# First layer norm of the experts' half: contiguous rows, one token tile at a time through its own banks, router by tile

## The reference

```
mix = hybrid_mixer(x, ...)                                  # three kinds of attention, then w_o
x   = layer_norm(ALPHA * x + mix, ln1_g, ln1_b)             # the first norm: this is what is changed
lg  = x @ router_group_w + b;   le = x @ router_expert_w + b   # 4 + 32 = 36 logits a token
...                                                         # best group, its two best experts, gates
moe = sum over chosen experts of (silu(x @ w_gate) * (x @ w_up)) * gate @ w_down
x   = layer_norm(ALPHA * x + moe, ln2_g, ln2_b)
```

## Time and profile before

| | |
|---|---|
| median of three runs | 1674.71 us |
| profiled execution, first to last instruction (its span; its own time is given only as this) | 1670.3 us |
| PE busy | 1640.6 us, 98% |
| PE weight loads busy | 1241.8 us, 74% |
| DVE busy | 856.1 us, 51% |
| ACT busy | 651.0 us, 39% |
| POOL busy | 172.6 us, 10% |
| mean granted TensorE clock | 0.996 of full speed |

### The profile page before, as it was taken

How to read it: one execution, slowest core, us unless ns; L and a number is a source line. 1 busy time by engine, 2 the same in 40 slices (tenths; PEclk the granted TensorE clock), 3 DMA queues, 4 the chain that set the end, 5 groups by cost and what they waited for, 6 DMA issues and landing times. The chain is left out here.

```text
span 1670.3 us, 23474 instructions
## 1 busy us (share of the span) xinstructions
PE 1640.6 (98%) x9386; PEld 1241.8 (74%) x9386; DVE 856.1 (51%) x1420; ACT 651.0 (39%) x920; POOL 172.6 (10%) x242
## 2 busy tenths in 40 slices
PE   9999999999999999999999999999999999999997
PEld 7888879999798887999988976444448887544443
DVE  6566564444646556544456867322117785532223
ACT  5455444343445454433345453111115455211111
POOL 2020001111102100111111040000002022000000
PEclk9999999999999999999999999999999999999999
DMA  9544545553654455465546546999996637699996
GB/s 324 184 140 151 177 152 182 196 178 124 229 181 146 151 176 177 153 199 177 180 157 196 189 142 230 406 422 420 421 392 211 193 126 250 228 421 421 421 417 260
DMA packets 158589, 396.61 MB, mean 237 GB/s; under 512 B 20753, under 2 KB 85265, under 8 KB 140049
## 3 DMA queue, kind: packets, MB, share of 16 engines
q1 hardware_dynamic: 158480, 395.18, 65.0%
HBM read 394.10 MB, written 1.05 MB: 237 GB/s over the span
## 5 line engine op out<-in xcount | busy, mean ns | idle before, releaser
L948 PE MATMUL ps<-split,split 128*128 128x256 f32 (+3 forms) x1872 | 631.7, 337 | 0.6 <-issue 0.3
L952 PE MATMUL ps<-split,split 128*128 128x256 f32 (+3 forms) x1872 | 627.8, 335 | 0.6 <-DVE split L2707 0.6
L949 PE MATMUL ps<-split,split 128*128 128x256 f32 (+3 forms) x1872 | 623.9, 333 | 0.0
L926 DVE TENSOR_TENSOR split<-ring,split 128x2048 fp32r<-128x2048 f32 x136 | 312.5, 2305 | 254.0 <-ACT split L919 253.9
L952 PEld LDWEIGHTS ps<-split,split 128*128 128x128 f32 x1872 | 352.0, 188 | 36.1 <-DVE split L2412 1.1
L948 PEld LDWEIGHTS ps<-split,split 128*128 128x128 f32 x1872 | 351.8, 188 | 35.3 <-issue 2.4
L949 PEld LDWEIGHTS ps<-split,split 128*128 128x128 f32 x1872 | 353.2, 189 | 33.0 <-issue 0.5
L919 ACT ACTIVATE split<-ring 128x2048 fp32r<-128x2048 f32 x136 | 260.3, 1915 | 278.0 <-PE ps L952 267.8
L1874 PE MATMUL ps<-ring,arena 128*64 128x512 f32 x464 | 105.8, 592 | 0.3 <-DMA ring<-in_expert_w_up 0.3
L3068 DVE SCALAR_TENSOR_TENSOR arena<-arena,ps 128x256 f32<-128x256 f32 x32 | 15.4, 480 | 171.7 <-ACT arena L2327 136.0
L1874 PE MATMUL ps<-arena 128*64 128x512 f32 x288 | 99.5, 594 | 0.0
(11 more groups left out here) (260 smaller groups left out, 1690.5 us busy)
## 6 DMA issues: line engine op xcount, KB each, us to landing
ring<-in_w_in SPq DMA_DIRECT2D x52, 1024.0 KB, 5.1
ring<-in_w_gate_up SPq DMA_DIRECT2D x44, 1024.0 KB, 5.3
ring<-in_expert_w_down SPq DMA_DIRECT2D x32, 1024.0 KB, 13.2
ring<-in_w_down SPq DMA_DIRECT2D x22, 1024.0 KB, 5.0
ring<-in_w_in SPq DMA_DIRECT2D x28, 768.0 KB, 4.5
ring<-in_expert_w_gate SPq DMA_DIRECT2D x20, 1024.0 KB, 11.9
ring<-in_expert_w_up SPq DMA_DIRECT2D x20, 1024.0 KB, 14.0
arena<-in_expert_w_down SPq DMA_DIRECT2D x16, 1024.0 KB, 14.5
```

The source lines that it names most:

```text
L926: nc.vector.tensor_tensor(split(slot), slot, split(high[:, n % HIGH, :]), ALU.subtract).then_inc(low_done.sem, 1)
L948: nc.tensor.matmul(acc, sh, mh, start=start, stop=False)
L949: nc.tensor.matmul(acc, *second, start=False, stop=False)
L952: return nc.tensor.matmul(acc, *third, start=False, stop=stop)
```

## The change

`Z` is now written as it is read, row for row, without the step of eight. The step is moved to where PE reads `Z`, `H_high` and `H_low` as stationary operands (`k::KT`), in the transposes and in the gathers. Each token tile is turned into four banks of its own (4 to 7 for tile 0, 1 to 4 for tile 1), the blocks are taken out 128 columns at a time, and the router takes the tiles one after the other. A table `Z_BY` says which engine takes which block: ACT (0) takes k = 0 to 5 of tile 0 and k = 2, 3, 6, 7 of tile 1, DVE (1) the rest. PE runs 6 filler matmuls instead of 16, and its order becomes: turn tile 0, router for blocks 0 to 5 of tile 0, turn tile 1, router for blocks 6 and 7 of tile 0, router for tile 1. `shift` is computed on POOL. In DVE's queue the memsets and the two blocks of tile 0 stand ahead of the normalisation of tile 1; in ACT's queue the six blocks of tile 0 stand ahead of the split of `Z[:, 0]`. The residual in duos 1 and 3 loses its step.

```diff
+Z_BY = ((0, 0, 0, 0, 0, 0, 1, 1), (1, 1, 0, 0, 1, 1, 0, 0))
...
-    out += [(("xT2", kp), 4 + kp) for kp in range(4)] + [(("router", 0), 0), (("ranks", 0), 1)]
+    out += [(("xT2", 0, kp), 4 + kp) for kp in range(4)] + [(("xT2", 1, kp), 1 + kp) for kp in range(4)]
+    out += [(("router", 0), 0), (("ranks", 0), 1)]
...
+            def turn_z(t, l):
+                done = (z_act, z_dve)[t]
+                pe.wait_ge(done.sem, done.at(l, 1))
+                for k in range(KT):
+                    key = ("xT2", t, k // 2)
+                    acc = claim2(key, l) if k % 2 == 0 else bank2(key)
+                    mm = nc.tensor.transpose(acc[:, k % 2 * P:(k % 2 + 1) * P], Z[:, t, k::KT], ident[:])
+                    if k % 2 == 1:
+                        fill(mm, key)
+            def route(t, first, last, l):
+                acc = bank2(("router", 0))
+                for k in range(first, last + 1):
+                    engine, n = z_block(t, k)
+                    signal_ = (xT2_act, xT2_dve)[engine]
+                    pe.wait_ge(signal_.sem, signal_.at(l, n))
+                    mm = nc.tensor.matmul(acc[:, t * 64:t * 64 + 36], T8[:, k, t * P:(t + 1) * P], rw[:, k, :],
+                                          start=(t == 0 and k == 0), stop=(t == TT - 1 and k == KT - 1))
...
-                keep_running(bank2(("xT2", 3)), 16)
-                turn_z(l)
-                (router: for each k the matmuls of both tiles)
+                keep_running(bank2(("xT2", 0, 3)), 6)
+                turn_z(0, l)
+                route(0, 0, 5, l)
+                turn_z(1, l)
+                route(0, 6, 7, l)
+                route(1, 0, 7, l)
...
-                                                      moe_split((H_high, H_low)[part][:, t, k * P:(k + 1) * P]),
+                                                      moe_split((H_high, H_low)[part][:, t, k::KT]),
...
-                nc.scalar.activation(in_blocks(Z[:, 0, :]), H[:, 0, :].rearrange("p (n k) -> p k n", k=KT), ACT.Identity,
-                                     scale=rstd2[:, 0:1], bias=shift[:, 0:1]).then_inc(z_act.sem, 1)
+                nc.scalar.activation(Z[:, 0, :], H[:, 0, :], ACT.Identity, scale=rstd2[:, 0:1],
+                                     bias=shift[:, 0:1]).then_inc(z_act.sem, 1)
+                leave_z(0)
                 act.wait_ge(z_act.sem, z_act.at(l, 1))
                 high_of_z(0)
-                (the blocks k = 0, 1, 4, 5 of both tiles)
+                leave_z(1)
...
-                    if i == 3:
-                        dve.wait_ge(rstd_done.sem, rstd_done.at(l, 1))
-                        nc.vector.scalar_tensor_tensor(out=shift, in0=mv2[:, 0, 0:1], scalar=-1.0, in1=rstd2[:, 0:1],
-                                                       op0=ALU.mult, op1=ALU.mult).then_inc(shift_in.sem, 1)
...
+                (memsets)
+                leave_z(0)
+                dve.wait_ge(rstd_done.sem, rstd_done.at(l, 2))
+                nc.vector.tensor_scalar(Z[:, 1, :], H[:, 1, :], mv2[:, 1, 0:1], rstd2[:, 1:2], ALU.subtract,
+                                        ALU.mult).then_inc(z_dve.sem, 1)
+                leave_z(1)
+                low_of_z(0)
...
-                                out=H[:, d // 2, :].rearrange("p (n k) -> p n k", k=KT),
-                                in0=Z[:, d // 2, :].rearrange("p (k n) -> p n k", k=KT), scalar=ALPHA,
-                                in1=lng[:, 0, :].rearrange("p (n k) -> p n k", k=KT), op0=ALU.mult,
+                                out=H[:, d // 2, :], in0=Z[:, d // 2, :], scalar=ALPHA, in1=lng[:, 0, :], op0=ALU.mult,
...
+                    if t == 0:
+                        pool.wait_ge(rstd_done.sem, rstd_done.at(l, 1))
+                        nc.gpsimd.tensor_scalar(shift, mv2[:, 0, 0:1], rstd2[:, 0:1], -1.0, ALU.mult,
+                                                ALU.mult).then_inc(shift_in.sem, 1)
```

More of the change, by code:

```diff
@@ L273, in gathers_in, with z_block @@
     return [(g, n)] if group_parts(g) == 4 else [(g, 2 * n), (g, 2 * n + 1)]
+def z_block(t, k):
+    engine = Z_BY[t][k]
+    return engine, sum(Z_BY[i][j] == engine for i in range(TT) for j in range(KT) if (i, j) <= (t, k))
 def gather_banks(d):
@@ L697, in build @@
         bT_low = signal("bT_low", 16)
-        xT2_act = signal("xT2_act", 4)
-        xT2_dve = signal("xT2_dve", 4)
+        xT2_act = signal("xT2_act", sum(row.count(0) for row in Z_BY))
+        xT2_dve = signal("xT2_dve", sum(row.count(1) for row in Z_BY))
         u_act = signal("u_act", 10)
@@ L767, in wait_apart @@
             eng.sem_inc(passed, 1)
-        def in_blocks(view):
-            return view.rearrange("p (k n) -> p k n", k=KT)
         def bank_of(key):
@@ L809, in build @@
             read2["xT", kp] = (bT_low, kp + 5)
-            read2["xT2", kp] = ((xT2_act, xT2_dve)[kp % 2], 2 * (kp // 2) + 2)
+            for t in range(TT):
+                engine, n = z_block(t, 2 * kp + 1)
+                read2["xT2", t, kp] = ((xT2_act, xT2_dve)[engine], n)
             read2["uq", kp] = (mq_in, kp + 1)
@@ L1588, in turn_stream @@
                             fill(mm, ("xT", b))
[L1590 to L1599, removed]
+            def turn_z(t, l):
[15 more added lines that the diff above has]
+                                          start=(t == 0 and k == 0), stop=(t == TT - 1 and k == KT - 1))
+                if t == TT - 1:
+                    fill(mm, ("router", 0))
             def index_scores(h, l):
@@ L2280, in high_of_z, with leave_z @@
                     nc.scalar.activation(moe_split(H_high[:, t, :]), Z[:, t, :], ACT.Copy).then_inc(split_high.sem, 1)
+                def leave_z(t):
+                    for k in range(KT):
+                        engine, _ = z_block(t, k)
+                        if engine == 0:
+                            acc = content2(("xT2", t, k // 2), l)
+                            nc.scalar.activation(T8[:, k, t * P:(t + 1) * P], acc[:, k % 2 * P:(k % 2 + 1) * P],
+                                                 ACT.Identity, scale=ln1_of_d[:, 0, k:k + 1],
+                                                 bias=ln1_of_d[:, 1, k:k + 1]).then_inc(xT2_act.sem, 1)
                 act.wait_ge(shift_in.sem, shift_in.at(l, 1))
-                nc.scalar.activation(in_blocks(Z[:, 0, :]), H[:, 0, :].rearrange("p (n k) -> p k n", k=KT), ACT.Identity,
-                                     scale=rstd2[:, 0:1], bias=shift[:, 0:1]).then_inc(z_act.sem, 1)
+                nc.scalar.activation(Z[:, 0, :], H[:, 0, :], ACT.Identity, scale=rstd2[:, 0:1],
+                                     bias=shift[:, 0:1]).then_inc(z_act.sem, 1)
+                leave_z(0)
                 act.wait_ge(z_act.sem, z_act.at(l, 1))
                 high_of_z(0)
[L2287 to L2290, removed]
+                leave_z(1)
                 act.wait_ge(z_dve.sem, z_dve.at(l, 1))
@@ L2927, in _, with leave_z @@
                                                 ALU.add).then_inc(stat_done.sem, 1)
[L2928 to L2935 removed]
+                def leave_z(t):
+                    for k in range(KT):
+                        engine, _ = z_block(t, k)
+                        if engine == 1:
+                            acc = content2(("xT2", t, k // 2), l)
+                            nc.vector.tensor_scalar(T8[:, k, t * P:(t + 1) * P], acc[:, k % 2 * P:(k % 2 + 1) * P],
+                                                    ln1_of_d[:, 0, k:k + 1], ln1_of_d[:, 1, k:k + 1], ALU.mult,
+                                                    ALU.add).then_inc(xT2_dve.sem, 1)
                 nc.vector.memset(minus_mean, -1.0 / D)
```

20 lines of the change are left out of this document (3 added, 17 removed).

## The result

| | before | after |
|---|---|---|
| median | 1674.71 us (1673.34 to 1675.06, 5 runs) | 1707.08 us (1704.22 to 1710.50, 5 runs) |
| span of the profiled execution | 1670.3 us | 1702.4 us |
| mean granted clock | 0.996 | 0.990 |

The change made the kernel slower, by the ratio 1.0196, 95% interval 1.0185 to 1.0208: 32.4 us where 2.0 us were to be won.

A forecast was written before the change was run, and what follows sets the result against it. PE, busy 98% of the span, was taken as the bound, with DMA also full in the duos. Router 1.23 us sooner less 0.2 for gathers: 1.0 a layer, 2.0 in both, 1674.7 - 2.0 = 1672.7 us; range 1670.9 to 1675.4.

The forecast's parts named there:

- Gathers with a step of eight: PE's gathers reading weights with a step: 32 narrow ones on the path cost nothing to 0.6 us a layer, 0.2 taken.
- Rival A: The step slows PE's gathers by x us each; 1679.2 us with the longer load, about 1699 if the rate halves; 5%.
- the halving: PE's gather rate halves under the step as ACT's does, x = 0.12: 12 us a layer, about 1699 us; one percent.
- Rival B: Low clock comes in both layers and falls on the first duo, losing 1.7 us each: 1676.1 us; 7%.
- Shift on POOL: Normalisation of tile 0: shift computed on POOL is ready at 7.37, so ACT can start at 7.40 instead of 8.26.
- rows without a step: ACT's normalisation of tile 0 read and written contiguously takes 1.2 us instead of 2.23; tile 1's on DVE 0.85.
- transposes: PE's transposes of Z with a step of eight stay about as fast, 0.124 us apart.
- blocks: ACT takes out six 128-column blocks of tile 0, 0.355 us apart, done at 11.37; DVE's two are done at 10.77.
- router: PE's router instructions, 0.112 us apart, end at 15.05 instead of 16.28: 1.23 us sooner a layer.
- D: Rival: PE hardly waits for ACT's 128-column blocks (distance nearer 0.25 than 0.355 us), gain 3.5 to 4.2, about 1670.9 us; 13%.
- I take the shift of the first gather as the shift of the layer's end: Time won before the gathers reaches the layer's end in full, once per layer, the DMA stretch moving along.
- Hidden: DVE's residual in duos 1 and 3 loses its step, without effect on the time, as DVE is busy 47 of 196 us.

The follow-up runs named there:

- e1: The changed kernel with the gathers' stationary operands contiguous again (wrong columns, same sizes): 1675.67 us, ratio 1.0003 to the kernel before.
- e2: The kernel before with only a step of eight put into the gathers' stationary operands (wrong columns): 1709.29 us, ratio 1.0213 to the kernel before.
- e3: The changed kernel with the step of eight only in each layer's first 32 narrow gathers, later ones contiguous: 1687.67 us, ratio 1.0078 to the kernel before.
- e5: The changed kernel with a step of four instead of eight in the gathers' weights (wrong columns): 1704.53 us, ratio 1.0178 to the kernel before.
- e6: The changed kernel with both halves written in column blocks, the high one by ACT, so gathers are contiguous and right: 1680.94 us, ratio 1.0041 to before.
- e7: The changed kernel with halves written in column blocks, the high one by POOL instead of ACT, gathers contiguous and right: 1678.85 us, ratio 1.0029 to before.
- g1: The changed kernel, but rows normalised in blocks as before, gathers contiguous and right, ten fillers, other DVE order: 1677.31 us, ratio 1.0018 to before.
- the small kernel: Separate kernel, run once, with groups of 24 matmuls varying type and step of the weights: fp32r at 160 columns, step 8, takes 5.96 us.

## Why the prediction was wrong, point by point

- **The step that failed** is "*Gathers with a step of eight*": "The nearest rows for the step are again the transposes, where it adds 0.002 to 0.019 to the distance ... I take 0.2". The mechanism was named there, that the weight load sets the distance; its rate under a step was taken from rows that do not show it. It adds 0.135 us at 160 columns and 0.249 - 0.151 = 0.098 at 320 (20 in 5.16 us against 3.19). The rows of the load itself were among those read, 198 ns against 141, and were called latency. In the gathers the same reading went from 190 to 335 ns.
- **Rival A** had it: with x = 0.12 "about 1699". With the measured 0.135 and 0.098 the same sum is 32 x 0.135 + 96 x 0.098 + 32 x 0.135 = 18.0 a layer, less 1.3 won and the waits of 1.7 and 2.4 us taken back: some 29.5 in both, 1704. The low clock in the first duos, 2.4 in both, and the 2 us between the layers come on top and would make 1708 to 1709; 1707.08 was measured. Its "covered up to about 2 us by the wait for DMA" held. The weight of one in a hundred on the halving was wrong, against a row of ACT that showed it and the rule of the Trainium skill that the prediction itself names; the prediction let one kind of PE instruction speak for another.
- **Rival B** had the low clock in both layers and in the first duo. It came, for 10 us and not 3.4, and with e1 it went. The four profiles whose first gathers are slow (the changed kernel, e2, e3, e5) have it at them in both layers, for 7 to 10 us; of the ten others it stands at the first gathers in three of 20 layers (e6, e7, g1). So the slow gathers bring it, though they are not the only thing that does. It cost 1.1 to 1.3 a layer, nearly all of it behind the gathers, for with a step of eight these are no slower at 1.2 GHz (0.248) than those of the small kernel at full clock (0.247). In e2, where the clock falls in the middle of them, they start 0.242 us apart at full clock and 0.241 at half. This holds for the slow load alone: contiguous gathers start 0.113 apart at full clock and 0.214 at half (g1). Without the step the low clock still came more often, and there it took gain.
- **Shift on POOL, rows without a step, transposes, blocks, router**: right to 0.1 us each on PE's path; 1.23 forecast, 1.30 measured. ACT's row at 128 columns, where D had its hope, was as computed: six in 2.20 against 2.23.
- **"I take the shift of the first gather as the shift of the layer's end"**: right for a delay (e3), and not so for a gain. "If PE is earlier, the releases are" did not hold in full, since e1's waits for weights grew by 1.2 us; and it left out that a stage can be shorter and still bring the low clock oftener. In e1 this took the gain (1675.67 against the 1672.7 forecast); in the changed kernel the step decided.
- **Hidden**: the residual fell from 1956 to 1215 ns a row, and nothing else moved with it, as said.

## What to carry to other kernels

A layout change moves a step from one reader to another, so price it at every reader, and at TensorE price the load of the weights and not only the matmul: ask at each matmul whether the load or the columns set the distance. Where the nearest row is of another kind of instruction, a minute with a small kernel that varies only the step would have told a loss of 2% from a gain of 0.1%. When a gain of a microsecond doesn't arrive, sort single runs by their granted clock as well as looking for a new wait.

## What the runs showed of the hardware that was not expected

- The load of 128 x 128 fp32r weights takes 0.118 us contiguous, 0.126 at step 2, 0.181 at 3, 0.244 at 4 and 0.247 at 8; 24 bf16 loads with 64 columns each take 0.86 us contiguous and at step 2, 0.95 at step 4, 1.61 at step 8. Transposes of fp32 blocks stay at 0.11 to 0.12 whatever the step (24 in 2.78 to 3.06 us), and matmuls of 512 columns hide it.
- Matmuls of 160 columns with a contiguous load start 0.113 us apart at full clock and 0.214 at half; with a step of eight it is 0.242 and 0.241.
- Plain fp32 matmuls with 36 columns slow down as well: 48 take 6.45 us contiguous and 11.43 at step 8 (mean clock 0.83 and 0.65 in these rows).
- A step of 16 was a little faster than one of 8 or 4 (5.48 against 5.96 and 5.89 us), for which I have no reading.
- For 1024 columns, ACT writing with a step of 128 elements took 2.07 us against 1.08 in order, and DVE reading one operand and writing with that step 1.94 against 1.22.
- POOL's cast of 1024 columns more than doubled a DVE normalisation beside it, 0.81 to 1.98 us.
